# Compressing cache rows: a feature-major copy in SBUF between the loaded rows and TensorE, keys and values in turn

## The chip, the cores and the metric

The kernel runs on one core of a Trainium2 chip. The metric is the device time of one execution in microseconds; before the change it is 1770.71 us, the median of three runs (1770.42 to 1772.65). The profile shows one further execution.

## The reference

One inference step of a two-layer decoder: a prompt of 512 tokens and 8 sample tokens with 2048 past positions each share all weights. Layer 0 is sparse attention with three branches (compressed blocks, selected blocks, a window), layer 1 gated linear attention; each is followed by a SwiGLU feed-forward. The part at hand is the compression of the cached rows of the 8 samples. Each cached row holds 4 heads of 64 features for keys and as many for values; 64 consecutive rows make a block, and each block is reduced to one row a head:

```python
def compress_blocks(rows, pe, w1, w2):
    B, L = rows.shape[:2]
    nb = L // CMP_BLK                                   # CMP_BLK = 64
    blk = rows[:, :nb * CMP_BLK].reshape(B, nb, CMP_BLK, 2, NSA_KV_HEADS, NSA_HEAD_DIM)
    h = jax.nn.silu(jnp.einsum('bnlcgd,lcde->bncge', blk + pe[:, :, None, :], w1))
    return jnp.einsum('bncge,cef->bncgf', h, w2)

# for each sample: 2048 rows gathered by page_table, 16 pages of 128 rows
cmp_past = cache_cmp_kv[li, page_table].reshape(B, past_len, 2, G, D)
ckv = concatenate([compress_blocks(cmp_past, pe, w1, w2), compress_blocks(cmp_kv, pe, w1, w2)])
```

The prompt's own rows (8 blocks) are compressed with the same weights. The results feed a small attention, whose probabilities also choose the selected blocks.

## The kernel before

Phases follow one another, each a block of instruction streams, one for each engine, with semaphores between them: the projection (`phase_project`), the compression (`phase_compress`), the attention over compressed rows (`phase_cmp_attention`), the selected and window attention (`phase_attention`), then the trunk of layer 0, layer 1 and its trunk. At the end of a block all engines meet.

The compression has 128 pages (8 samples of 16), each with keys and values. It works in eight units `UN`: 32 pages (`ROW_UNIT`) of keys four times, then 32 pages of values four times. A page of one kind is 128 rows of 256 floats: position in the partition, 1 KB a partition and page. A unit is 32 such pages side by side. TensorE multiplies, for each of the 64 features d, the 64 positions of a block (in partitions 0 to 63 and, for the second block of a page, 64 to 127) by the 64x64 weights `w1[:, c, d]`, and adds over d in PSUM. The moving operand for one d is one element of each page and head: 128 columns which lie 64 floats apart (`flat`, line 704). Features 0 to 31 go to one half of the output partitions and 32 to 63 to the other (`far`), blocks to two banks (`hf`), so that four 64x64 matmuls stand in four tiles of the array at a time. A unit is 32 steps of four matmuls (256 records in the trace, since a float32 matmul shows as two). Some units carry extra columns: four for the position row `pe`, in the first unit of keys and of values (132), 16 for the prompt's rows, in the second of each (144, with the unused four).

Two row buffers alternate: `rows0`, whose first 32 pages are loaded during the projection, and a second. The load of unit n + 2 waits for `conv_done` of unit n. The 32 page DMAs are issued by SyncE (13), ScalarE (10) and GpSimd (9) (`ROW_SHARE`), each with a page number read from the page table into a register (`row_pages`, line 105), for each unit anew.

After a unit VectorE adds the two halves and the position term (`other`, `pre`), ScalarE takes the sigmoid (`sig`), VectorE multiplies (`hid`). Within the last unit's convolution, between steps of TensorE, the prompt's blocks are finished: second weights for them (`new_blocks`), `prompt_values`, `prompt_scores`, `turn_scores`, and on VectorE the prompt's softmax (`prompt_softmax`), which there stands ahead of the last unit's activation. The product of all `hid` with the second weights `w2` (line 718) ends the phase.

`xT`, the transposed input of 128 x 8 x 520 floats (2.13 MB), stays in SBUF through all of this, from the projection to the trunk of layer 0, though no phase between reads it. In the projection weights stream through four slots `raw`; SyncE's queue issues them, and GpSimd's `low_done` frees a slot.

## Time and profile before

| what | value |
|---|---|
| median of three runs | 1770.71 us |
| the profiled execution | 1766.21 us, of it a span of 1764.5 us |
| mean granted clock of TensorE over the span | 0.959 |
| first convolution matmul of the compression | 173.96 us after the span's start |
| first product with the second weights | 314.09 us |
| first matmul of the compressed attention | 317.35 us |
| TensorE busy over the span | 92% |

The profile's times count from the span's start. "PE" is TensorE's matmuls, "PEld" its weight loads, DVE VectorE, ACT ScalarE, POOL GpSimd, SP SyncE; a "q" behind an engine is its instruction queue. "L709" is a line of the kernel. In a timeline, neighbouring instructions of one line are merged, and the bracket says how long the engine was idle before them and what released it. The granted clock is a share of 2.4 GHz and takes two levels, 1.00 and 0.50 (1.2 GHz).

### The profile page before, as it was taken

To read this page: it belongs to the slowest core of one execution; us is meant where nothing else is said; L and a number is where in the kernel's file an instruction comes from. 1 tells how busy PE (TensorE), PEld (TensorE's weight loads), DVE (VectorE), ACT (ScalarE), POOL (GpSimd) and SP (SyncE) were. 2 spreads that over 40 slices of the span, in tenths; PEclk is the share of its full clock that TensorE was granted. 3 is DMA by queue.
4 is the path that set the end of the run, shared out by engine and by line. 5 is a ranking of instruction groups with operands and counts; after the bars stand their busy time and mean duration, and the time that the engine had idled before them with its cause. 6 is when DMAs were issued, how large, how long until landed. Compare 5 with 4: busy or idle time off the path is not lost. (4 is left out here: it accounts for less than half of the span.)

```text
span 1764.5 us, 35479 instructions
## 1 busy us (share of the span) xinstructions
PE 1631.3 (92%) x13658; PEld 1429.0 (81%) x13658; DVE 729.4 (41%) x1364; ACT 577.6 (33%) x1142; POOL 723.1 (41%) x503
## 2 busy tenths in 40 slices
PE   6998889698899888999999999998979999999997
PEld 6998777476666677999999988987658899999996
DVE  2111011555455669332232267136659523223234
ACT  3221001255454435422222224126534532222323
POOL 6641231343255446644344336412126644434420
PEclk9999999799999999999999999998979999999998
DMA  8326885255454543533333222324223333333211
GB/s 211 103 80 170 282 271 162 75 181 155 139 162 149 152 120 120 167 120 108 110 119 96 84 64 69 99 83 155 61 71 109 96 110 93 91 89 99 85 32 49
DMA packets 297280, 211.42 MB, mean 120 GB/s; under 512 B 34148, under 2 KB 290328, under 8 KB 296600
## 3 DMA queue, kind: packets, MB, share of 16 engines
q1 hardware_dynamic: 279000, 175.69, 33.4%
q0 software_dynamic: 7552, 20.06, 3.6%
q10 hardware_dynamic: 10560, 13.41, 2.8%
q8 instruction: 109, 1.79, 0.4%
q14 instruction: 59, 0.48, 0.1%
HBM read 199.02 MB, written 18.42 MB: 123 GB/s over the span
## 5 line engine op out<-in xcount | busy, mean ns | idle before, releaser
L1670 POOL TENSOR_TENSOR w_low_t<-w_raw,w_high_t 128x1024 fp32r<-128x1024 f32 (+1 forms) x126 | 298.7, 2380 | 296.3 <-ACT w_high_t L1778 296.3
L1511 PE MATMUL ps<-x_parts,w_high_t 128*128 128x512 f32 x720 | 262.5, 403 | 16.3 <-POOL w_low_t L1670 15.7
L1758 PE MATMUL ps<-x_parts,w_high_t 128*128 128x264 f32 x720 | 205.1, 285 | 0.0
L1760 PE MATMUL ps<-x_parts,w_low_t 128*128 128x264 f32 x720 | 204.4, 284 | 0.0
L1759 PE MATMUL ps<-x_parts,w_high_t 128*128 128x264 f32 x720 | 204.4, 284 | 0.0
L1513 PE MATMUL ps<-x_parts,w_low_t 128*128 128x256 f32 x720 | 204.3, 284 | 0.0
L1511 PEld LDWEIGHTS ps<-x_parts,w_high_t 128*128 128x128 f32 x720 | 138.2, 192 | 47.9 <-POOL w_low_t L1670 16.5
L1778 ACT CAST w_high_t<-w_raw 128x1024 fp32r<-128x1024 f32 (+1 forms) x126 | 127.9, 1024 | 135.6 <-PE ps L1760 118.3
L1670 POOL TENSOR_TENSOR w_low_ahead<-w_raw,w_high_ahead 128x1024 fp32r<-128x1024 f32 (+1 forms) x40 | 95.1, 2380 | 132.2 <-ACT w_high_ahead L1778 132.2
L1513 PEld LDWEIGHTS ps<-x_parts,w_low_t 128*128 128x128 f32 x720 | 138.5, 192 | 0.1
L1758 PEld LDWEIGHTS ps<-x_parts,w_high_t 128*128 128x128 f32 x720 | 135.4, 188 | 2.9
L1759 PEld LDWEIGHTS ps<-x_parts,w_high_t 128*128 128x128 f32 x720 | 135.4, 188 | 0.1
L1760 PEld LDWEIGHTS ps<-x_parts,w_low_t 128*128 128x128 f32 x720 | 135.3, 188 | 0.0
L709 PE MATMUL ps<-rows,w 64*64 64x128 f32 (+2 forms) x2048 | 118.3, 401 | 17.7 <-DMA rows<-in_cache_cmp 12.3
L709 PEld LDWEIGHTS ps<-rows,w 64*64 64x64 f32 x2048 | 97.7, 157 | 37.8 <-issue 15.1
L1078 POOL TENSOR_TENSOR e<-e,rg 128x1024 f32<-128x1024 f32 (+3 forms) x48 | 66.9, 1394 | 113.4 <-DVE rg L1332 113.0
L1912 DVE TENSOR_REDUCE whole_t<-ps 128x256 f32<-128x512 f32 x44 | 30.4, 690 | 181.4 <-PE ps L1513 181.4
L328 PE MATMUL ps<-x_parts,pw_high 128*128 128x260 f32 x320 | 93.4, 292 | 5.2 <-POOL pw_low L248 5.2
L1795 ACT CAST hid_parts<-h_t 128x256 fp32r<-128x256 f32 (+1 forms) x88 | 36.1, 410 | 186.3 <-DVE h_t L1917 186.3
L1511 PE MATMUL ps<-hid_parts,w_high_t 128*128 128x512 f32 x264 | 93.8, 395 | 0.0
L329 PE MATMUL ps<-x_parts,pw_high 128*128 128x260 f32 x320 | 91.0, 284 | 0.0
L330 PE MATMUL ps<-x_parts,pw_low 128*128 128x260 f32 x320 | 90.6, 283 | 0.0
(392 smaller groups left out, 3914.0 us busy)
## 6 DMA issues: line engine op xcount, KB each, us to landing
w_raw<-in_ffn_w_gu SPq DMA_DIRECT2D x88, 512.0 KB, 3.7
pages<-in_cache_slc SPq DMA_DIRECT2D x192, 128.0 KB
rows<-in_cache_cmp SPq DMA_DIRECT2D x123, 128.0 KB, 5.5
w_raw<-in_ffn_w_down SPq DMA_DIRECT2D x32, 448.0 KB, 3.7
w_raw<-in_gla_w_in SPq DMA_DIRECT2D x24, 512.0 KB, 3.7
rows<-in_cache_cmp ACTq DMA_DIRECT2D x70, 128.0 KB, 6.2
pages<-in_cache_slc POOLq DMA_DIRECT2D x64, 128.0 KB, 2.9
w_raw<-in_ffn_w_down SPq DMA_DIRECT2D x16, 512.0 KB, 4.0
```

The lines of the kernel that those rows point to most:

```text
L328: nc.tensor.matmul(out, high[:, u % SLOTS, k, :], X[0][:, k, c], start=(k == 0), stop=False)
L329: nc.tensor.matmul(out, high[:, u % SLOTS, k, :], X[1][:, k, c], start=False, stop=False)
L330: ins = nc.tensor.matmul(out, low[:, u % SLOTS, k, :], X[0][:, k, c], start=False, stop=(k == KT - 1))
L709: ins = nc.tensor.matmul(ps[64 * far:64 * far + 64, 2 * (n % 2) + hf, 0:m * G], w1[half, c, d + D // 2 * far, :], flat[half, d + D // 2 * ...
L1078: nc.gpsimd.tensor_tensor(part, part, rg[:, n % 4].unsqueeze(2).to_broadcast([P, 2, w]), ALU.mult)\
L1511: nc.tensor.matmul(bank[:, 0:2 * FOLD].rearrange("p (a n) -> p a n", a=2), high, parts[2][:, :, at, 0:FOLD], start=(k == 0), stop=False)
L1513: return nc.tensor.matmul(bank[:, FOLD:2 * FOLD], low, parts[0][:, at, 0:FOLD], start=False, stop=(k == n - 1))
L1670: nc.gpsimd.tensor_tensor(low(u)[:, 0:k], raw[:, u % RAW, 0:k], high(u)[:, 0:k].bitcast(F32), ALU.subtract).then_inc(low_done, 1)
L1758: nc.tensor.matmul(psum(i), high(u)[:, k, :], a[0][:, at, c], start=(k == 0), stop=False)
L1759: nc.tensor.matmul(psum(i), high(u)[:, k, :], a[1][:, at, c], start=False, stop=False)
L1760: ins = nc.tensor.matmul(psum(i), low(u)[:, k, :], a[0][:, at, c], start=False, stop=(k == t.kc - 1))
L1778: nc.scalar.copy(high(u)[:, 0:k], raw[:, u % RAW, 0:k]).then_inc(high_done, 1)
```

## The change

Between the row buffers and TensorE stands a ring of four small tiles `flat`. ScalarE and VectorE in turn copy chunks into it: a chunk is 4 features of each half for all 128 columns, feature outermost, so that the columns of one feature are neighbours. A unit has 8 chunks (`CH`, a local name here); even ones are ScalarE's, odd ones VectorE's (`flatten`). TensorE waits for each chunk and releases it with `chunk_done`. Prompt rows and position rows are copied into the chunks of the first two units by the same engines, as 16 columns and one.

The order of units is keys, values, keys, values of the same pages, so page numbers are read once for two units. A row buffer is free when all its chunks are copied. The shares of the page issues are 14, 6 and 12. ScalarE's issues of its part stand behind its copies of a unit. VectorE's work on unit n - 1 stands among its copies for unit n, and the prompt's work is spread over units 3 to 6.

Three of the four ring tiles lie where `xT` was. So `xT` is written to DRAM (`x_saved`) in the projection, behind the issue of the fifth unit's weights, and read back at the end of the attention's page loads, ahead of the trunk's first weights on the same queue.

```diff
-ROW_SHARE = (0, 13, 23, ROW_UNIT)
+ROW_SHARE = (0, 14, 20, ROW_UNIT)
@@ phase_project, SyncE: in the loop over weight units u
                 if u == SPREAD0 - 1:
+                    sp.wait_ge(xT_done, 2 * NT)
+                    sp.dma_start(S["x_saved"], xT[:].rearrange("p k t -> p (k t)")).then_inc(xT_saved, 16)
                     sp.wait_ge(pt_in, 16)
-                    for hf in range(2):
-                        sp.dma_start(S["rows0"][64 * hf:64 * hf + 64, 32], io["nsa_pe_cmp"][0, :, 0, :].unsqueeze(1)
-                                     .to_broadcast([BLK, G, D])).then_inc(cst["rows0_in"], 16)
@@ phase_project, ScalarE: behind the loads of w1
+            for c in range(2):
+                for hf in range(2):
+                    act.dma_start(S["pe_cmp"][64 * hf:64 * hf + 64, c], io["nsa_pe_cmp"][0, :, c, :]).then_inc(cst["rows0_in"], 16)
@@ phase_compress
-    UN = [(c, p) for c in range(2) for p in range(PARTS)]
-    EX = (1, PARTS + 1)
+    UN = [(c, p) for p in range(PARTS) for c in range(2)]
+    EX = (0, 1)
+    PEC = COLS + XC
+    CD, RING = 4, 4
+    CH = D // 2 // CD
@@ load_part
             if n >= 2:
-                eng.wait_ge(conv_done, n - 1)
+                eng.wait_ge(flat_act, CH // 2 * (n - 1))
+                eng.wait_ge(flat_dve, CH // 2 * (n - 1))
...
+            if n % 2 and n + 1 < len(UN):
+                S["next_pages"][by] = row_pages(eng, S, (n + 1) // 2, by)
+        def flatten(eng, copy, n, j, done):
+            c, k = UN[n][0], CH * n + j
+            dst = flat[k % RING]
+            if j < 2:
+                rows_there(eng, n)
+            if k >= RING:
+                eng.wait_ge(chunk_done, k - RING + 1)
+            if n in EX:
+                for f in range(2):
+                    src = S["cmpn"][:, 0:TILES, c * G * D:(c + 1) * G * D].rearrange("p t (g e) -> p e t g", g=G)
+                    copy(dst[:, f, :, COLS:COLS + XC].rearrange("p e (t g) -> p e t g", g=G),
+                         src[:, f * (D // 2) + CD * j:f * (D // 2) + CD * (j + 1)])
+                copy(dst[:, :, :, PEC], S["pe_cmp"][:, c].rearrange("p (f e) -> p f e", f=2)[:, :, CD * j:CD * (j + 1)])
+            src = rows[n % 2][:].rearrange("p s g (f e) -> p f e (s g)", f=2)
+            copy(dst[:, :, :, 0:COLS], src[:, :, CD * j:CD * (j + 1), :]).then_inc(done, 1)
@@ ScalarE
+            for n in range(len(UN)):
+                for j in range(0, CH, 2):
+                    flatten(act, nc.scalar.copy, n, j, flat_act)
+                    if j == 2 and n:
+                        sigmoid(n - 1)
+                if n == 6:
+                    act.wait_ge(e_ready, 1)
+                    nc.scalar.activation(sp_[:], sp_[:], ACT.Exp, scale=SCALE).then_inc(e_done, 1)
+                if n == 0:
+                    load_part(act, 1, 1, rows_act)
+                    for c in range(2):
+                        act.dma_start(w2[64 * c:64 * c + 64], io["nsa_w_cmp2"][0, c]).then_inc(w2_in, 16)
+                    for name in ("pm_add", "pm_01"):
+                        act.dma_start(S[name][:], io[name + "_tab"]).then_inc(pm_in, 16)
+                if n + 2 < len(UN):
+                    load_part(act, n + 2, 1, rows_act)
+                if n == 4:
+                    act.wait_ge(cst["cmp_out"], 16 * 4)
+                    act.wait_ge(flat_dve, CH // 2 * len(EX))
                     for g in range(G):
                         act.wait_ge(sT_done, g // 2 + 1)
                         nc.scalar.copy(sT[:, g], ps[:, 4 + g, :]).then_inc(sT_ready, 1)
+            sigmoid(len(UN) - 1)
@@ VectorE
+            for n in range(len(UN)):
+                for j in range(1, CH, 2):
+                    flatten(dve, nc.vector.tensor_copy, n, j, flat_dve)
+                    if j == 1 and n:
+                        activate(n - 1)
+                    if j == 3 and n:
+                        finish(n - 1)
+                    if j == 3 and n == 4:
+                        new_values()
+                if n == 3:
+                    new_keys()
+                if n == 5:
+                    shift_scores()
+                if n == 6:
+                    prompt_softmax()
@@ TensorE
+            beside = {(3, 4): new_blocks, (4, 0): prompt_values, (4, 6): prompt_scores, (5, 2): turn_scores}
             for n, (c, p) in enumerate(UN):
...
+                for j in range(CH):
+                    k = CH * n + j
+                    if (n, j) in beside:
+                        beside[n, j]()
+                    pe.wait_ge(flat_dve if j % 2 else flat_act, k // 2 + 1)
+                    for e in range(CD):
+                        for far in range(2):
+                            for hf in range(2):
+                                half = slice(64 * hf, 64 * hf + 64)
+                                ins = nc.tensor.matmul(ps[64 * far:64 * far + 64, 2 * (n % 2) + hf, 0:m],
+                                                       w1[half, c, CD * j + e + D // 2 * far, :], flat[k % RING][half, far, e, 0:m],
+                                                       start=(j == 0 and e == 0), stop=(j == CH - 1 and e == CD - 1),
+                                                       tile_position=(64 * hf, 64 * far))
+                    ins.then_inc(chunk_done, 1)
@@ phase_attention, SyncE: behind all page loads
+            sp.dma_start(S["xT"][:].rearrange("p k t -> p (k t)"), S["x_saved"]).then_inc(xT_back, 16)
             sp.wait_ge(sc_done, NK)
             for u in range(RAW):
                 load_unit(sp, cst["raw"], cst["w_in"]["t0"], u, next_units[u])
+            sp.wait_ge(xT_back, 16)
```

SyncE now issues the tables behind all of its page loads. `activate` and `finish` are the two halves of the former work after a unit; their operations are the same.

## Rows read from the trace of the kernel before

**Rows 1.** The page: busy time, share of the span and instructions of each engine.

```profile
PE 1631.3 (92%) x13658; PEld 1429.0 (81%) x13658; DVE 729.4 (41%) x1364; ACT 577.6 (33%) x1142; POOL 723.1 (41%) x503
```

**Rows 2.** Timeline of TensorE, 173 to 315 us: start, length, operation, count, idle before.

```profile
173.96 14.60 PE L709 MATMUL ps<-rows,w 64*64 64x132 f32 x256 [3.33 <-PEq L123]
195.45 29.90 PE L709 MATMUL ps<-rows,w 64*64 64x144 f32 x512 [6.89 <-DMA rows<-in_cache_cmp]
...
227.83 14.17 PE L709 MATMUL ps<-rows,w 64*64 64x128 f32 x256 [2.48 <-DMA rows<-in_cache_cmp]
...
243.45 14.66 PE L709 MATMUL ps<-rows,w 64*64 64x132 f32 x256 [1.45 <-DMA rows<-in_nsa_pe_cmp]
...
258.78 15.87 PE L709 MATMUL ps<-rows,w 64*64 64x144 f32 x256 [0.67 <-issue]
...
291.83 1.99 PE L709 MATMUL ps<-rows,w 64*64 64x128 f32 x32 [2.46 <-DMA rows<-in_cache_cmp]
...
305.15 5.44 PE L709 MATMUL ps<-rows,w 64*64 64x128 f32 x96
314.09 1.61 PE L718 MATMUL ps<-hid,w 64*64 64x512 f32 x8 [3.50 <-DVE hid L644]
```

**Rows 3.** Windows: length, busy time (records) of PE to POOL, granted clock, DMA.

```profile
197.00:198.00 1.00, 1.00 (x24) 1.00 (x20) 0.00 (x0) 0.00 (x0) 0.00 (x0) 0.50 1.10 366
...
200.00:201.00 1.00, 1.00 (x24) 0.87 (x20) 0.00 (x0) 0.00 (x0) 0.00 (x0) 1.00 1.03 325
```

**Rows 4.** Windows of line 718: length, PE, PEld, clock, DMA share, GB/s.

```profile
314.10:314.15 0.05, 0.05 (x4) 0.05 (x6) 1.00 0.00 0
...
314.50:314.55 0.05, 0.05 (x4) 0.00 (x0) 0.73 0.00 0
...
314.60:314.65 0.05, 0.05 (x8) 0.00 (x0) 0.50 0.00 0
```

**Rows 5.** DMA view of 173.8 to 195.4 us; timeline of ScalarE's queue.

```profile
DMA packets 5949, 7.11 MB, mean 329 GB/s; under 512 B 870, under 2 KB 5495, under 8 KB 5909
...
211.59 6.05 ACTq L504 DMA_DIRECT2D rows<-in_cache_cmp  x10
```

**Rows 6.** Groups by line and form: count, busy us, mean ns, idle before.

```profile
L352 ACT CAST pw_high<-w_raw 128x1024 fp32r<-128x1024 f32 x20 | 21.0, 1052 | 1.2 <-DMA w_raw<-in_nsa_w_in 1.2
...
L623 DVE COPY rows<-cmpn 128x256 f32<-128x256 f32 x8 | 1.8, 284 | 0.6 <-PEq L123 0.6
...
L434 DVE COPY qs<-qT 64x32 f32<-64x32 f32 x8 | 1.1, 185 | 0.0
```

**Rows 7.** Line 105: duration min/median/max ns; timeline of the queue of ScalarE.

```profile
L105 ACTq TENSOR_LOAD <-pt x70: 271/275/714, 159.1 to 269.9; - x70
L105 ACTq FUSED_REGOPS  x70: 147/147/170, 159.8 to 270.2; - x70
...
179.12 3.68 ACTq L547 DMA_DIRECT2D w<-in_nsa_w_cmp  x2
```

**Rows 8.** Timeline of VectorE at the phase's end.

```profile
311.46 0.69 DVE L610 TENSOR_TENSOR p_cmp<-p_cmp,sm_p 128x512 f32<-128x512 f32 x1
312.19 0.42 DVE L633 COPY c_other<-ps 64x256 f32<-64x256 f32 x1
```

**Rows 9.** The projection: windows; timelines of SyncE's queue and of ScalarE.

```profile
24.00:28.00 4.00, 4.00 (x33) 4.00 (x33) 0.00 (x0) 0.00 (x0) 4.00 (x5) 0.95 1.08 346
...
40.00:44.00 4.00, 4.00 (x32) 3.88 (x31) 1.40 (x2) 1.54 (x2) 1.51 (x2) 1.00 0.65 193
...
27.22 1.01 SPq L209 DMA_DIRECT2D w_raw<-in_nsa_w_in  x2
...
41.67 1.05 ACT L352 CAST pw_high<-w_raw 128x1024 fp32r<-128x1024 f32 x1
```

**Rows 10.** The attention's end: timeline of SyncE's queue; tile w_raw, 560 to 660 us.

```profile
589.04 51.20 SPq L1525 DMA_DIRECT2D w_raw<-in_nsa_w_out  x32
...
L1778 ACT CAST w_high_t<-w_raw x7: 1030/1040/1050, 625.5 to 659.8; 128x1024 fp32r<-128x1024 f32 x7
```

More of the change, by code:

```diff
@@ L237, in _ @@
             sp.wait_ge(kv_out, 16 * 8)
+            sp.wait_ge(xT_saved, 16)
         @block.gpsimd
@@ L468, in sem @@
             return cst["sems"].new(name)
-        rows = (S["rows0"], sb("rows", [P, QP + EXTRA, G, D]))
+        rows = (S["rows0"], sb("rows", [P, QP, G, D]))
+        flat = [nc.alloc_sbuf_tensor_at("flat%d" % i, [P, 2, CD, WIDE], F32, offset=S["xT_at"] + 8 * CD * WIDE * i)
+                for i in range(RING - 1)] + [sb("flat%d" % (RING - 1), [P, 2, CD, WIDE])]
         w1 = S["w1"]
```

160 lines of the change are left out of this document (63 added, 97 removed).

## The prediction

> **What bounds the kernel now.** I read the page's shares first: TensorE is busy for 92% of the span [rows 1], but that is an average over phases. The change touches one, the compression, so I took the timeline of that stretch next. TensorE's first convolution matmul there starts at 173.96 us, the last ends at 305.15 + 5.44 = 310.6, and the product with the second weights, which ends the phase for TensorE, starts at 314.09 [rows 2]. So the phase lasts 140.1 us. A unit (32 pages of keys or of values) takes 14.2 us with 128 columns, 14.6 with 132, 15.9 with 144; between units TensorE waits 6.89, 2.48, 1.45, 0.67 and 2.46 us, mostly for rows from DRAM (the second and third units follow without a wait, the seventh nearly so) [rows 2]. TensorE is thus busy most of the phase, and some 14 us are waits.
>
> Is a unit's 14.2 us bounded by TensorE's clock? Each float32 matmul shows as two records, so a unit is 256 records, or 64 groups of four that lie in four different 64x64 tiles of the array. A group takes 14.2 / 64 = 222 ns with 128 columns and 15.87 / 64 = 248 ns with 144: 1.6 ns for each further column, and nearly nothing left over. So columns set the pace, not weight loads. But the pace doesn't follow the clock: at a granted clock of 0.50 (1.2 GHz) as many matmuls are in flight per microsecond as at 1.00 (2.4 GHz), 24 and 24 [rows 3], and the second unit, which began at the low clock, took 29.90 - 14.2 = 15.7 us against 15.87 for its like at the full one [rows 2]. What streams is the strided operand: neighbours lie 64 floats apart. The same 64x64 tiling with a contiguous operand stands at the phase's end, 512 columns: four matmuls are in flight from 314.10 to 314.55 and eight, the next four with them, from 314.60, nearly all of it at the full clock [rows 4]. That is 0.45 to 0.5 us for 512 columns, 0.88 to 0.98 ns a column, about half of 1.7. So the bound is the strided read, and reading contiguously at the full clock should give 113 to 125 ns a group, 7.2 to 8.0 us a unit. At the low clock it doubles the 0.88, but no more than the present 14.2, since the rows of the strided form at that clock already hold that pace.
>
> The Trainium skill (SBUF — State Buffer, the note on cachelines in the section on the DMA port swizzle) says that accesses which each touch a new 16-byte line pay a penalty. By that rule the trace's 222 ns are explained; it gives no size for float32 on TensorE, so the sum goes by the rows above.
>
> **The change, step by step.**
>
> *TensorE's columns.* Both first units now carry 145 columns; of the others none exceeds 128. At the present pace this is 2 x 145 + 6 x 128 against 2 x 132 + 2 x 144 + 4 x 128: 1058 against 1064 columns, nothing. With the halved cost, units fall from 14.2 to between 7.2 and 14.2 us. After a wait the clock is low at first (it was 0.50 from before the second unit's start until about 198.5 [rows 3]), for 3 us at least; with half of that lost I take 9.5 us.
>
> *DMA becomes the pace.* A unit is 32 pages of 131 KB, 4.19 MB. In the stretch from 173.8 to 195.4 the DMAs moved 7.11 MB at 329 GB/s [rows 5], which gives 12.7 us for a unit with the queues full. A unit's load that stands alone, with its ramp, took from 211.59 (ACT's first issue) to 227.83 (TensorE's start), 16.2 us, some 0.5 MB of tables in it [rows 2, 5]. Now loads hardly overlap, since a buffer is free only when the unit's convolution is over. Afterwards a buffer is free when its rows are in the ring, which runs up to four of eight chunks ahead, and the other load is then under way. I take 13.5 us a unit when two loads overlap and 15 for one alone; the ends are 12.7 and 16.2.
>
> *The copies.* A chunk is 1024 elements a partition. ScalarE's nearest row is the cast of 1024 contiguous ones, 1.05 us; VectorE copied 256 within SBUF in 0.28 us and moves 32 strided ones in 0.185 [rows 6]. A strided copy of 1024 isn't shown: from below 1.05 us; from above twice that, if the stride costs it what it costs TensorE. Four chunks per engine and unit are 4.2 to 8.4 us, beside TensorE and the loads. I take 1.1 (ScalarE's pace of about 1 ns an element leaves more room than TensorE's). In the first two units two or three small copies are added to each chunk, 0.2 us each: 1.7.
>
> *ScalarE's queue.* This is where the change adds waits. ScalarE copies even chunks, and its six page issues of the load after next stand between its copies of one unit and of the next. Ten issues took 6.05 us [rows 5], so six take about 3.5; six page numbers take 0.275 + 0.147 us and gaps each [rows 7], 3.3 in all, now once in two units. If ScalarE is late, the next unit's first chunk is, and TensorE behind it. In the first unit it is worst: its part of load 1 was issued at 173.9, and now comes only behind its copies; then come two w2 issues (3.68 us before [rows 7]), two mask tables and its part of load 2, before it may copy a row of unit 1.
>
> *The walk.* Unit 0: first chunk at 175.6, and ScalarE's last copy (it needs TensorE to be through chunk 2, at the low clock) ends at 182.5. Then 3.5 + 3.3 + 3.7 + 3.7 + 3.5 gives 200.2 for the first copy of unit 1, while TensorE, done at about 185, waits 16 us (6.9 before). Copies of unit 1 end 8.5 us later, 208.7; ScalarE is through with its issues at 215.5, where unit 2's copies start (its rows, issued by 200, are there), ending at 222.5. Load 3 started at 208.7 and lands at 223.7; unit 3 starts at 226. Load 4 started at 222.5 and lands at 237.5; loads 5, 6 and 7 follow by 13.5 us: 278. Then 1.1 for a copy and 9.5 for TensorE: 288.6, where before it was 310.6. TensorE's side work (new blocks, prompt scores, turning), which lengthened the last unit to 310.6 - 291.8 = 18.8 us, lies in waits of the fourth to sixth units and costs nothing; without that cover it is 18.8 - 14.2 = 4.6 us.
>
> *The tail.* The softmax held VectorE until 312.15, so the last activation began 1.6 us after TensorE's end; then come 1.9 us until 314.09 [rows 8]. Now the softmax is over a unit earlier: 288.6 + 2.0 = 290.6. Gain: 314.1 - 290.6 = 23.5 us.
>
> *x to DRAM and back.* 2.13 MB, 6.5 us at 329 GB/s, each way. Out: behind the fifth unit's weights at 22.5 us, in a stretch where DMA is nearly full (1.08 between 24 and 28) and has room only later (0.65 between 40 and 44). The sixth unit's weights were issued at 27.22 and ScalarE took them up at 41.67, 14 us later [rows 9]; 6.5 us fit in, and the two broadcasts of position rows are gone. Without that cover it costs up to 6.5. Back: queued behind the last pages at 589 us, ahead of weights that are first read at 625.5 [rows 10]: hidden. Four small issues on ScalarE in the projection replace four page numbers. I put 0.3 us for all of it.
>
> *The sum.* The profiled run took 1766.2 us, its span 1764.5. 1766.2 - 23.5 + 0.3 = 1743; the median of the three runs is 4.5 us above the profiled one, so 1770.7 - 23.2 = 1747.5, rounded to 1747.
>
> **Rivals.**
>
> *TensorE stays at 14.2 us a unit.* For it: no row shows eight instructions in 115 ns over a long run, and a TensorE that waits between units may spend them at the low clock, where 128 contiguous columns take what they take now. Then unit 1 starts at 201 and ends at 217; six more, 85, and 4.6 of side work give 307, with the tail 309: a gain of 5, 1766 us. Against it: four 64x64 matmuls started together in rows 4. The Trainium skill (TensorE: Matmul & The Clock Gate, the section on HAM oscillation) warns of just this, DMA waits between bursts that put the clock down each time; here it would give the 1766, and the rows of the low clock after the 6.89 us wait agree that the clock falls.
>
> *Copies or ScalarE's queue set the pace.* At 2.1 us a copy ScalarE needs 8.4 + 3.5 + 1.7 + 0.5 for a unit, 14.1, and copies wait on chunks on top; with 15 us a unit from 222 the end comes at 222 + 5 x 15 + 11 = 308 at worst, 300 if half overlaps: 6 to 14 us, about 1760.
>
> *Slower.* One mechanism: the copy out of the strided rows costs 3 us or more, because VectorE and ScalarE pay the stride harder than TensorE. Then 12 + 5.7 = 17.7 us a unit, over the present 16.3 to 16.8 between starts: 200 + 7 x 17.7 + 4 = 328, 14 us slower, 1785. It decides from about 2.7 us a copy. The 0.185 us for 32 strided elements speaks against it, since most of that is fixed.
>
> *Nothing is left.* The first rival with x's way out uncovered: 5 us gained and up to 6.5 lost, 1771 at most and within 0.2%.
>
> **How the numbers follow.** Forecast 57%, 1747, its own range 1738 (12.7 us a load) to 1756 (16.2 for some of them). TensorE unchanged 15%, 1766. Copies or queue 16%, 1760. Slower 6%. Cancelling 6%. A measurement here can tell about 0.2%, 3.5 us. Faster by more than that: 0.87; within: 0.07; slower: 0.06. The range that leaves out 2 in 10 goes from 1736 to 1766.
>
> **What would show it.** Right: convolution units of 7 to 10.5 us of TensorE time; waits between units that end on copies, which waited for rows; DMA share near 1 from 222 on; a first wait of TensorE of some 15 us; the second-weights product some 117 us after 173.9, not 140. Wrong: units of 13 us or more; ScalarE's copies of 2 us; TensorE in the projection waiting for weights near 40 us; a later start of the trunk's first product.

## The result, and the profile after

The changed kernel takes 1759.65 us (median of 5 runs, 1755.05 to 1766.01) where the kernel before takes 1770.71 (5 runs, 1769.48 to 1772.65): a ratio of 0.9943, 95% interval 0.9926 to 0.996. That is 11.1 us faster, less than half of the 23.7 that were forecast, and it is the time of the rival "copies or ScalarE's queue set the pace", 1760, which had been given 16%. The profiled execution took 1758.1 us with a span of 1756.4, so the two profiles differ by 8.1 us, three less than the medians do.

TensorE's share falls by one point from that in [rows 1], its busy time by 38 us:

```profile
PE 1593.4 (91%) x13658; PEld 1407.0 (80%) x13658; DVE 757.8 (43%) x1412; ACT 643.3 (37%) x1198; POOL 740.8 (42%) x522
```

The timeline of TensorE through the compression, which answers to [rows 2] (start, length, operation, count, idle before):

```profile
183.68 9.88 PE L755 MATMUL ps<-flat,w 64*64 64x145 f32 x256 [12.46 <-ACT flat L539]
204.39 9.77 PE L755 MATMUL ps<-flat,w 64*64 64x145 f32 x256 [10.82 <-ACT flat L539]
220.35 9.89 PE L755 MATMUL ps<-flat,w 64*64 64x128 f32 x256 [6.19 <-ACT flat L539]
...
290.06 5.21 PE L755 MATMUL ps<-flat,w 64*64 64x128 f32 x128 [1.55 <-ACT flat L539]
295.52 3.89 PE L755 MATMUL ps<-flat,w 64*64 64x128 f32 x128 [0.26 <-ACT flat L539]
301.38 1.09 PE L765 MATMUL ps<-hid,w 64*64 64x512 f32 x8 [1.97 <-DVE hid L675]
```

A run of 256 records is again a unit. It now takes 9.8 to 9.9 us, and 128 records at the full clock take 3.89, which makes 3.89 / 32 = 122 ns a group of four records in place of 222 (the prediction's group is four records; a step of four matmuls is eight): the halving came as forecast. But each unit waits, and on a copy, not on rows. The product with the second weights stands at 301.38 where it was at 314.09: 12.7 us of the forecast 23.5. The reason is seen on ScalarE. Its timeline over the same stretch, where `ACTq` is its queue of DMA issues:

```profile
181.10 0.50 ACT L535 COPY flat<-cmpn 128x64 f32<-128x64 f32 x2 [9.90 <-DMA pe_cmp<-in_nsa_pe_cmp]
...
201.84 0.49 ACT L535 COPY flat<-cmpn 128x64 f32<-128x64 f32 x2 [10.61 <-issue]
...
211.96 2.96 ACTq L511 DMA_DIRECT2D rows<-in_cache_cmp  x6
218.30 3.77 ACT L539 COPY flat<-rows 128x1024 f32<-128x1024 f32 x2 [6.50 <-issue]
...
227.63 3.82 ACTq L511 DMA_DIRECT2D rows<-in_cache_cmp  x6
231.64 3.82 ACT L539 COPY flat<-rows 128x1024 f32<-128x1024 f32 x2 [4.17 <-issue]
...
287.98 3.85 ACT L539 COPY flat<-rows 128x1024 f32<-128x1024 f32 x2 [1.58 <-DMA rows<-in_cache_cmp]
```

Two copies together take 3.77 to 3.85 us in these rows. With units counted from 0 to 7: behind the fourth copy of a unit, ScalarE issues six pages of the load after next (3 to 4 us), reads page numbers in every second unit, and only then starts on the next unit. So its first copies of units 2 and 3 come at 218.30 and 231.64, with idle times that end on "issue" and not on rows. Between its first copies of unit 1 and of unit 7 it waited for rows once, for 1.58 us. It also waited for TensorE and VectorE there, 4.04 us in unit 4 (for the prompt's scores) and 3.57 at the start of unit 6; of 6.79 idle us ahead of unit 4, which the view puts down to TensorE, half are page numbers. The copies by line and form, ScalarE's and VectorE's of the same shape and the same number (count, busy us, mean ns, idle before):

```profile
L539 ACT COPY flat<-rows 128x1024 f32<-128x1024 f32 x32 | 62.4, 1973 | 27.6 <-PE ps L755 11.7 <-issue 10.7 <-DVE flat L539 3.6
...
L539 DVE COPY flat<-rows 128x1024 f32<-128x1024 f32 x32 | 33.9, 1058 | 18.5 <-PE ps L755 14.2 <-DMA rows<-in_cache_cmp 4.2
```

1973 ns on ScalarE, 1058 on VectorE. And the windows of that stretch, in which the DMA share (last but one column, the granted clock ahead of it) should have been near 1 from 222 us on:

```profile
201.00:208.00 7.00, 3.61 (x64) 3.64 (x68) 0.52 (x2) 6.17 (x13) 0.00 (x0) 0.51 1.03 337
...
222.00:229.00 7.00, 6.93 (x197) 6.68 (x193) 3.02 (x5) 4.50 (x4) 0.84 (x2) 0.79 0.66 205
...
236.00:243.00 7.00, 4.60 (x145) 4.26 (x141) 3.10 (x9) 3.56 (x2) 2.61 (x5) 0.92 1.06 349
```

It is 0.66 at 222 to 229 and 1.06 at 236 to 243, falls to 0.74 at 250 to 257 again, and its mean from 222 to 278 is 0.88, for the loads start when the copies are through and these are late. The first unit began late as well: 181.10 against the forecast 175.6. The tile with the rows of positions, its issues and landings:

```profile
L385 ACTq DMA_DIRECT2D pe_cmp<-in_nsa_pe_cmp x4: 618/618/628, 160.0 to 162.0; - x4
...
DMA to landing us min/median/max: 19.0/19.2/19.8
```

They are issued at 160.0 to 162.0 on ScalarE's queue behind the first weights, 4.2 MB, and land 19 us later.

**Behind the phase** part of the gain goes again. "The trunk's second layer" is here the first product that reads the hidden values of the trunk's feed-forward (`hid_parts`). The start of TensorE's same matmuls in the two profiles, before against after: product with the second weights 314.09 and 301.38 (12.7 us earlier); the attention's last product 622.75 and 612.09 (10.7); the trunk's first 629.04 and 618.68 (10.4); the trunk's second layer 775.54 and 767.98 (7.6); the end 8.1. Attention has one new wait, 1.2 us for pages of the window cache; such waits come and go, kernel 1 below, without x's trip, has one of 1.4 us for other pages. The trunk's first layer, from its first product to the second layer's, takes 149.3 us in place of 146.5 and waits for nothing new. What differs is seen in windows around its longest wait, for the squares of the normalisation. Of before and after, first the timeline row of the wait, then windows of 3 us (length, PE, PEld, DVE, ACT, POOL, clock, DMA share, GB/s):

```profile
694.73 0.71 PE L1704 MATMUL ps<-ln_sq_t,mean_mat 128*128 128x264 f32 x2 [2.79 <-DVE ln_sq_t L1960]
```

```profile
692.00:695.00 3.00, 0.27 (x1) 0.27 (x2) 2.93 (x5) 0.00 (x0) 0.02 (x1) 1.00 0.77 227
695.00:698.00 3.00, 3.00 (x18) 2.58 (x18) 1.73 (x4) 2.03 (x3) 0.00 (x0) 1.00 0.04 10
```

```profile
685.59 1.19 PE L1753 MATMUL ps<-ln_sq_t,mean_mat 128*128 128x264 f32 x2 [2.81 <-DVE ln_sq_t L2009]
```

```profile
683.00:686.00 3.00, 0.41 (x1) 0.41 (x2) 2.93 (x5) 0.00 (x0) 0.00 (x0) 0.95 0.69 194
686.00:689.00 3.00, 3.00 (x10) 2.40 (x10) 1.59 (x4) 2.16 (x4) 0.00 (x0) 0.50 0.02 6
```

The wait is the same, 2.79 and 2.81 us. Before, the clock granted behind it is 1.00 and TensorE gets through 18 matmuls in 3 us; after, it is 0.50 (1.2 GHz) and 10 matmuls. So what differs behind this wait is the clock, not the work.

### The profile page after: what moved, and what is told of

Its sections match the earlier page's. It is cut to its first block and busy times, and to the rows that moved or that the text cites. A ratio compares the mean times of both kernels' runs of the same rounds, so it can differ in the third digit from the quotient of the medians.

```text
span 1756.4 us, 35338 instructions
## 1 busy us (share of the span) xinstructions
PE 1593.4 (91%) x13658; PEld 1407.0 (80%) x13658; DVE 757.8 (43%) x1412; ACT 643.3 (37%) x1198; POOL 740.8 (42%) x522
## 5 line engine op out<-in xcount | busy, mean ns | idle before, releaser
L1827 ACT CAST w_high_t<-w_raw 128x1024 fp32r<-128x1024 f32 (+1 forms) x126 | 127.9, 1024 | 136.6 <-PE ps L1809 118.3
L755 PE MATMUL ps<-flat,w 64*64 64x128 f32 (+1 forms) x2048 | 76.8, 314 | 47.5 <-ACT flat L539 43.7
L755 PEld LDWEIGHTS ps<-flat,w 64*64 64x64 f32 x2048 | 72.8, 158 | 51.8 <-issue 48.2
```

Of the source, the lines that this page charges most:

```text
L755: ins = nc.tensor.matmul(ps[64 * far:64 * far + 64, 2 * (n % 2) + hf, 0:m], w1[half, c, CD * j + e + D // 2 * far, :], flat[k % RING][half ...
L1827: nc.scalar.copy(high(u)[:, 0:k], raw[:, u % RAW, 0:k]).then_inc(high_done, 1)
```

## The experiments

Each of the twelve kernels was timed beside the kernel before on the same chip, and the ratios are to that kernel before. Kernels 1 to 4, 5 to 8, 9 to 11, and 12 ran on four different chips, so kernels of different groups are compared by their ratios; 0.001 of a ratio is 1.8 us. "The product" is that with the second weights, at 314.09 us before and 301.38 after.

**1. The kernel before, read contiguously.** TensorE reads the rows where they lie, so the wrong elements meet the weights; sizes and counts are those of before.

```diff
-flat = rows[n % 2][:, 0:m].rearrange("p s g d -> p d (s g)")
+flat = rows[n % 2][:, 0:m].rearrange("p s g d -> p (s g d)")\
+    .rearrange("p (d x) -> p d x", d=D)
```

> The kernel before, with one edit: TensorE reads each unit's rows as if they lay feature by feature, so 128 contiguous floats where it read 128 floats 64 apart. The elements are the wrong ones for their feature (that part of the result is changed), the instructions, loads, buffers and waits are those of before. Theory A, the strided read is what bounds TensorE: a unit falls from 14.2 us to 7.2 at the full clock and 9 to 10 with the low clock after each wait; the loads then set the pace, and since a load only starts when the buffer's convolution is over, a pair of units takes a load (16 us) and a convolution (9 us) at least, so 13 us a unit and more; the phase (140 us) shrinks by 15 to 25 us. Rival B, TensorE's instructions or weight loads take 14 us anyway: units stay at 14 us and the phase at 140.

1763.49 us (6 runs), ratio 0.996, 0.9943 to 0.9977. Timeline of TensorE, all runs of 512 records:

```profile
200.38 17.10 PE L709 MATMUL ps<-rows,w 64*64 64x144 f32 x512 [15.19 <-DMA rows<-in_cache_cmp]
232.58 16.99 PE L709 MATMUL ps<-rows,w 64*64 64x128 f32 x512 [15.10 <-DMA rows<-in_cache_cmp]
264.94 16.83 PE L709 MATMUL ps<-rows,w 64*64 64x144 f32 x512 [15.38 <-DMA rows<-in_cache_cmp]
...
311.57 1.98 PE L718 MATMUL ps<-hid,w 64*64 64x512 f32 x8 [6.07 <-DVE hid L644]
```

Two units take 17 us where they took 28 to 30, in a kernel in which nothing else was touched: the strided read was the bound. But each pair now waits 15 us for rows, the pairs stand 32.3 us apart, and the product comes 2.5 us earlier, no more. The expectation had the phase shrink by 15 to 25 us, which missed. So halving TensorE's work alone is worth 7.5 us in the medians and 1.9 in the profiles' spans; a unit's load that starts when TensorE is through with the buffer takes as long as before. What the ring adds to the faster read is that it lets the buffers go early.

**2. The trip of x alone.** The kernel before, with x saved to DRAM behind the fifth weight unit and fetched back ahead of the trunk's weights, as in the change.

```diff
 if u == SPREAD0 - 1:
+    sp.wait_ge(xT_done, 2 * NT)
+    sp.dma_start(S["x_saved"], xT[:]...).then_inc(xT_saved, 16)
...
     load(sp, i, range(SP_B), in_sp)
+sp.dma_start(S["xT"][:]..., S["x_saved"]).then_inc(xT_back, 16)
 sp.wait_ge(sc_done, NK)
```

> The kernel before, and only the way of x to DRAM and back is added, at the places where the change has it; x also stays in SBUF. Prediction: 0.3 us. Theory A, the trip costs what the trace of the changed kernel hints at behind the compression: 1 us of a late last window page in the attention and up to 3 us in the trunk's first units: 2 to 5 us slower than before. Rival B, it is hidden and those 4.6 us come from elsewhere: within 1 us of before.

1773.26 us (12 runs) against 1770.96 (25 runs), ratio 1.0014, 1.0004 to 1.0024: the trip costs 2.5 us, 0.7 to 4.2. I had put 0.3 for it. The two transfers of 2080 KB took 12.5 and 14.4 us here, not 6.5. In the one profile the product comes 3.6 us later than before, at 317.67, and the trunk's first layer takes 149.9 us for 146.5; its span is 7.4 us longer, three times what the medians say, so these parts are not the price of the trip one by one.

**3. The trip at another place.** The changed kernel, with the save behind the fourteenth weight unit and the fetch among attention's page loads.

```diff
-sp.wait_ge(xT_done, 2 * NT)
-sp.dma_start(S["x_saved"], ...)          # behind the fifth unit
+if u == 13:
+    sp.dma_start(S["x_saved"], ...)
...
 load(sp, i, range(SP_B), in_sp)
+if i == DEPTH + 4:
+    sp.dma_start(S["xT"][:]..., S["x_saved"])
```

> The changed kernel, with x written to DRAM behind the fourteenth weight unit instead of the fifth, and read back among the attention's page loads (behind the fifth load of that loop) instead of ahead of the trunk's first weights. If the trip as placed costs 3 to 5 us (theory A), this is 2 to 5 us faster than the changed kernel's 1759.65, about 1756; if it is hidden (rival B), 1759 to 1760.

1762.71 us (12 runs), ratio 0.9961, 0.9949 to 0.9972: no gain over the changed kernel, so moving the trip to this place saves nothing. The twelve runs tell something else. They go from 1753.95 us at a mean granted clock of 0.955 to 1769.0 at 0.942, and nearly in order (a correlation of -0.94 over the twelve), some 1.2 us for each 0.001 of the clock, 15.05 / 13. The 25 runs of the kernel before on that chip have clocks of 0.954 to 0.959 and times without such an order (-0.2). This is a correlation; no run here sets the clock by itself.

**4. The rows of positions ahead of the first weights**, in the changed kernel.

```diff
+for c in range(2):
+    for hf in range(2):
+        act.dma_start(S["pe_cmp"][...], io["nsa_pe_cmp"]...)
 for c in range(2):
     for hf in range(2):
         act.dma_start(w1[...], io["nsa_w_cmp1"]...)
```

> The changed kernel, with the four small loads of position rows issued on ScalarE's queue ahead of the four loads of the first weights (4.2 MB) instead of behind them. Theory A, the ring's first copies wait for the position rows because these stand behind all first weights: the first copy moves from 181.1 to about 175 us, the phase ends 6 us earlier, about 1754. Rival B, something behind it (the load of unit 1, ScalarE's queue) is due at the same time: the first convolution starts earlier and the second does not, under 2 us gained in all.

1759.6 us (6 runs), ratio 0.9937, 0.9919 to 0.9955: nothing. The first copy does come at 174.29 and TensorE starts 7 us earlier, at 176.87. Timeline of ScalarE, then of TensorE:

```profile
205.02 0.50 ACT L535 COPY flat<-cmpn 128x64 f32<-128x64 f32 x2 [20.42 <-DMA rows<-in_cache_cmp]
```

```profile
176.87 7.34 PE L755 MATMUL ps<-flat,w 64*64 64x145 f32 x163 [5.68 <-ACT flat L539]
...
207.60 10.07 PE L755 MATMUL ps<-flat,w 64*64 64x145 f32 x256 [19.27 <-ACT flat L539]
```

The second unit starts 3 us later than in the changed kernel. Its rows, ScalarE's six pages issued at 182.3 to 186.3, are there only at 205; the third unit's pages, let go by earlier copies, were by then under way as well (ScalarE's issued from 192.02 on, where the changed kernel has 197.54). The product stands at 305.70, 4.3 us later than in the changed kernel. The late rows of positions were an error of my walk, but not a cost.

**5. VectorE makes all copies**, ScalarE keeps the activations, its page numbers and its issues.

```diff
-for j in range(0, CH, 2):
-    flatten(act, nc.scalar.copy, n, j, flat_act)
-    if j == 2 and n:
-        sigmoid(n - 1)
+if n:
+    sigmoid(n - 1)
...
-for j in range(1, CH, 2):
+for j in range(CH):
     flatten(dve, nc.vector.tensor_copy, n, j, flat_dve)
```

> The changed kernel, with VectorE copying all eight chunks of a unit (1.06 us each in the changed kernel's trace) and ScalarE none (1.97 us each); ScalarE keeps its page issues, sigmoids and exponential. Theory A, ScalarE sets the pace of 14.3 us a unit with four copies, six issues and every second time six page numbers: units then follow at 13 us or less, TensorE's wait before unit 1 ends when its rows land (195.7 instead of 202), and the phase, which ends at 301.4 in the changed kernel, ends at 285 to 291; about 1747 us. Rival B, the loads set the pace: at most 3 us faster than the changed kernel's 1759.65.

1751.43 us (4 runs), ratio 0.9899, 0.9883 to 0.9916, clear of the changed kernel's 0.9926 to 0.996, though short of the 1747 expected. The product comes at 292.58, 21.5 us earlier than before and 2 us from the prediction's 290.6. Groups, then windows:

```profile
L538 DVE COPY flat<-rows 128x1024 f32<-128x1024 f32 x64 | 65.0, 1053 | 18.2 <-DMA rows<-in_cache_cmp 17.2 <-PE ps L752 0.9
```

```profile
215.00:222.00 7.00, 4.80 (x131) 4.08 (x126) 5.03 (x7) 0.00 (x0) 2.57 (x4) 0.90 1.05 350
222.00:229.00 7.00, 3.53 (x78) 3.31 (x74) 1.83 (x2) 0.00 (x0) 6.27 (x11) 0.74 1.04 329
```

VectorE alone copies a unit in 8 x 1.05 = 8.4 us, which is below what a load takes, and now waits for rows; the DMA share is 1.05 and 1.04 where the changed kernel has 1.00 and 0.66, and TensorE no longer waits over 5 us from the second unit on. The edit moves the sigmoid as well, which no longer stands behind copies: VectorE waited 25.9 us for it in the changed kernel (13.1 and 12.8) and waits 0.9 here. There is a price too: GpSimd's twelve page issues of a unit, which took 7.5 to 8.6 us from the first to the last, take 8.0 to 16.1 us; why is not shown. Taking half of the copies from an engine whose queue was full is worth more than sharing them out.

**6. ScalarE issues its pages later**, behind its second copy of the next unit, in the changed kernel.

```diff
     if j == 2 and n:
         sigmoid(n - 1)
+        if n + 1 < len(UN):
+            load_part(act, n + 1, 1, rows_act)
...
-if n + 2 < len(UN):
-    load_part(act, n + 2, 1, rows_act)
```

> The changed kernel, with ScalarE's page issues for the load after next standing behind its second copy of the next unit, not ahead of its first. Same work on ScalarE in another order. If ScalarE is saturated (theory A), TensorE's waits move into the unit and the pace stays at 14.3 us, within 2 us of the changed kernel. If only the order holds TensorE up (rival C), its waits of 2.5 to 6.2 us before units shrink to 1 to 2 and the phase ends 6 to 10 us earlier.

1755.03 us (4 runs), ratio 0.992, 0.9901 to 0.994, which overlaps the changed kernel's 0.9926 to 0.996. The product comes at 300.56, 0.8 us earlier. ScalarE's first copy of the second unit comes 4.8 us sooner (197.07 for 201.84), but in the units behind it the copies wait again on issue, 6.22 us before 220.82, and on late rows, 2.67 before 210.28: the queue is as full as before, only in another order.

**7. ScalarE copies contiguously**: its large copies read 1024 neighbours (the wrong elements), VectorE's stay strided.

```diff
+if j % 2 == 0:
+    src = rows[n % 2][:].rearrange("p s g d -> p (s g d)")\
+        .rearrange("p (f e x) -> p f e x", f=2, e=D // 2)
+else:
-src = rows[n % 2][:].rearrange("p s g (f e) -> p f e (s g)", f=2)
+    src = rows[n % 2][:].rearrange("p s g (f e) -> p f e (s g)", f=2)
```

> The changed kernel, with ScalarE's large copies reading their 1024 elements contiguously (the wrong elements, so half of the compressed sums are changed); VectorE's copies read as before. Theory A, the strided read doubles ScalarE's copy: 1.97 us falls to 1.05, four copies save 3.7 us a unit, and the pace falls from 14.3 to 12.7 to 13.5 us, the phase by 5 to 9 us. Rival: the 1.97 us come from something else (the four-dimensional shape, or the port shared with DMA writes): it stays above 1.5 us and nothing is gained.

1754.67 us (4 runs), ratio 0.9915, 0.9898 to 0.9931; this interval too touches the changed kernel's. Groups by line and form, then ScalarE's timeline:

```profile
L542 DVE COPY flat<-rows 128x1024 f32<-128x1024 f32 x32 | 33.9, 1060 | 29.5 <-PE ps L758 19.9 <-DMA rows<-in_cache_cmp 9.5
L542 ACT COPY flat<-rows 128x1024 f32<-128x1024 f32 x32 | 32.8, 1045 | 44.2 <-PE ps L758 20.3 <-issue 12.6 <-DMA rows<-in_cache_cmp 11.2
```

```profile
216.52 1.99 ACT L542 COPY flat<-rows 128x1024 f32<-128x1024 f32 x2 [7.40 <-issue]
...
229.45 1.99 ACT L542 COPY flat<-rows 128x1024 f32<-128x1024 f32 x2 [5.24 <-issue]
```

The same engine, size and destination take 1045 ns instead of 1973: the stride doubles ScalarE's copy. The product comes at 296.19, 5.2 us of the 8.8 that taking ScalarE's copies away brings. What is left is mostly the queue: 7.40 and 5.24 us of "issue" ahead of a unit's first copies, and from 216.52 to 229.45 a unit still takes 12.9 us.

**8. The same as 5, with pages shared 11, 11 and 10** among the queues of SyncE, ScalarE and GpSimd, not 14, 6 and 12.

```diff
-ROW_SHARE = (0, 14, 20, ROW_UNIT)
+ROW_SHARE = (0, 11, 22, ROW_UNIT)
```

> As e5_all_dve, and the page issues dealt as 11, 11 and 10 instead of 14, 6 and 12, since ScalarE has room. Theory A: once ScalarE's copies are gone the issue of 32 pages and the reading of page numbers are spread evenly, a load's last page is issued 2 us earlier, 0 to 4 us better than e5_all_dve. If the bytes alone bind then: the same as e5_all_dve.

1756.68 us (5 runs), ratio 0.9937, 0.9913 to 0.996, the product at 300.00: 7.4 us worse than kernel 5 in the phase; in the times the two intervals just touch. The pages do come sooner, and VectorE waits 7.1 us for rows where it waited 21.4. But it now waits for the sigmoid, which stands behind ScalarE's longer row of issues and page numbers. VectorE's waits from 176 to 300 us (what it waits for: us in total, times, longest):

```profile
DVE hid L672 <- ACT c_sig L563: 9.9, 5, 4.7
DVE hid L670 <- ACT c_sig L563: 7.7, 1, 7.7
```

That is 17.6 us where kernel 5 has 0.9. ScalarE's free time isn't worth giving to page issues as long as the sigmoid stands behind them; with the sigmoid ahead of them it wasn't tried.

**9 and 10. All copies on VectorE, and the rows of positions first**; in 10 the trip of x is also moved as in 3.

```diff
 (the edits of 5 and 4; in 10 those of 3 too)
```

> VectorE makes all copies, and the four rows of positions are loaded ahead of the first weights. Theory A (with ScalarE's copies gone, ScalarE's page numbers and issues of the second unit no longer stand behind copies, so the earlier start of the first unit is kept): the first copy moves from 180.3 to about 174 us and the second weights' product from 292.6 to 286-289; 1746 to 1749 us, a ratio of 0.986 to 0.988. Theory B (the loads set the pace of the whole phase, at about 330 GB/s from 205 us on, and nothing that starts earlier than them counts): the product stays at 291-294 and the time at 1750 to 1753 us, 0.989 to 0.990.

> The same as the last, and x is saved behind the fourteenth weight unit and fetched back among attention's page loads. Theory A (the fetch beside the trunk's first weights costs the trunk's first layer 3 us, as its distance from the trunk's first product to the second layer's first product says: 149.7 us against 146.5 before, and 146.6 where the trip was moved alone): that distance falls to 146.5 and the time lies 2 to 3 us below the last kernel's. Theory B (a fetch among attention's loads costs attention as much): the distance falls, but attention's 309.8 us from the second weights' product to its last product grow by 2 to 3 us, and the time is the last kernel's.

1762.18 us (6 runs), ratio 0.9947, 0.9929 to 0.9964, and 1764.05 us (11 runs), 0.9968, 0.9957 to 0.9979. The expectations missed: the edit that was worth nothing in 4 costs 8.5 us here by the ratios, 0.9947 for 0.9899 (10.8 by the medians of two chips), and 12.4 us in the phase. Timelines of kernel 9, VectorE and then TensorE:

```profile
204.14 0.36 DVE L534 COPY flat<-cmpn 128x64 f32<-128x64 f32 x2 [19.53 <-DMA rows<-in_cache_cmp]
```

```profile
205.66 6.49 PE L752 MATMUL ps<-flat,w 64*64 64x145 f32 x128 [18.60 <-DVE flat L538]
...
304.93 1.51 PE L762 MATMUL ps<-hid,w 64*64 64x512 f32 x8 [1.98 <-DVE hid L672]
```

The second unit's rows are there at 204, where kernel 5, which began 6 us later, had them at 195.12. The first unit's early end lets the third unit's pages in at once (ScalarE's at 184.78, in kernel 5 at 191.11), among the second's. The mean DMA share from 201 to 278 us is 0.84 for kernel 5's 0.95. In kernel 10 the product stands at 305.23 and the trunk's first layer takes 149.5 us, as without the move.

**11. ScalarE loads no pages** in the changed kernel; SyncE takes its six beside its fourteen.

```diff
-ROW_SHARE = (0, 14, 20, ROW_UNIT)
+ROW_SHARE = (0, 20, 20, ROW_UNIT)
```

> The kernel after, but ScalarE loads no pages of the compression: SyncE takes its six beside its fourteen. Theory A (ScalarE's queue of about 14 us a unit is 8 us of copies and some 6 of issues and page numbers, and both count): a unit falls to 10 to 12 us and the second weights' product comes at 285-293 us instead of 301.4; 1749 to 1754 us, a ratio of 0.988 to 0.991. Theory B (the transfers themselves, not their issue, set 13 us a unit once the issues are out of the way): the product comes at 296-301 us, and the time is 1754 to 1759 us, 0.991 to 0.994.

1768.84 us (10 runs), ratio 0.9991, 0.9981 to 1.0002: the whole gain is gone. Waits from 170 to 312 us (engine, tile and line, what it waits for: us in total, times, longest), then windows:

```profile
ACT flat L539 <- DMA rows<-in_cache_cmp: 48.2, 3, 18.2
DVE flat L539 <- DMA rows<-in_cache_cmp: 46.6, 3, 17.8
```

```profile
229.00:236.00 7.00, 7.00 (x259) 6.78 (x254) 5.03 (x7) 6.97 (x5) 4.66 (x5) 1.00 0.32 95
...
264.00:271.00 7.00, 5.76 (x171) 3.95 (x160) 3.32 (x5) 5.28 (x7) 4.90 (x8) 1.00 0.36 105
```

Neither expectation held. The issues left ScalarE, but the rows are late instead: both copying engines wait up to 18 us for them, every second unit, while the DMA engines stand at 0.32 and 0.36 between. SyncE's own program shows why. Its loads of page numbers in the first of these gaps (line 104; duration min/median/max ns, first and last start):

```profile
L104 SPq TENSOR_LOAD <-pt x20: 261/267/276, 228.4 to 239.2; - x20
```

Twenty page numbers take it 11 us, and it issues no page meanwhile. The forty issues of two units take 24.8 us, 203.2 to 228.0. That makes 36 us for two units, and two units do take 35.4, from 221.58 to 256.99, the first copies behind these waits. SyncE waits for nothing in this stretch, and its pages land 3.8 us behind their issue (median from 190 to 300 us), sooner than in the changed kernel (6.7). So it isn't that one queue brings twenty pages slowly: SyncE's turn of issues and page numbers, 18 us a unit, has become the pace, as ScalarE's was before. The issues were work that had to be dealt out; only ScalarE's copies could be taken away from it at a gain.

**12. Kernel 9, and the third unit's loads wait until the second's have landed.**

```diff
     eng.wait_ge(flat_dve, CH * (n - 1))
+if n == 2:
+    for q, arrived_q in enumerate((rows_sp, rows_act, rows_sw)):
+        eng.wait_ge(arrived_q[1], 16 * (SHARE[q + 1] - SHARE[q]))
```

> The kernel in which VectorE makes all copies and the rows of positions come ahead of the first weights (1762.2 us), with one edit: the loads of the third unit wait until those of the second have landed. Theory A (the earlier first unit let the third unit's pages into the queues while the second's were under way, and these landed at 203.7 us in place of 195, since both shared the DMA engines): the second unit's first copy comes at 190 to 196 us in place of 204.1, the second weights' product at 286 to 294 in place of 304.9; 1744 to 1752 us, a ratio of 0.985 to 0.990. Theory B (the second unit's pages are late because the first weights share the DMA engines with them, until about 182 us, and they would be so in any order): the first copy stays at 200 to 205 us, and the third unit's rows come later than before, so the product stands at 304 to 310; 1760 to 1766 us, 0.994 to 0.998.

1761.96 us (6 runs), ratio 0.9952, 0.994 to 0.9964. VectorE's timeline:

```profile
197.38 0.37 DVE L537 COPY flat<-cmpn 128x64 f32<-128x64 f32 x2 [12.63 <-DMA rows<-in_cache_cmp]
...
219.88 1.99 DVE L541 COPY flat<-rows 128x1024 f32<-128x1024 f32 x2 [10.04 <-DMA rows<-in_cache_cmp]
...
250.33 2.00 DVE L541 COPY flat<-rows 128x1024 f32<-128x1024 f32 x2 [10.25 <-DMA rows<-in_cache_cmp]
```

Half an answer. The second unit's rows are there at 197.38 and not at 204.14, so 6.8 us of the delay did come from the third unit's pages; the last 2 us to kernel 5's 195.12 didn't, and stay open. But the third unit's rows then come at 219.88, 22.5 us behind the second's, and the product stays at 304.86. From there on loads go out in pairs: GpSimd issues the 24 pages of two units in one go at 198.06, 230.58 and 260.81 us, where in kernel 5 it issues them twelve at a time, and VectorE waits 10.04, 10.25 and 6.37 us for the first unit of each pair and not for the second. The mean DMA share from 201 to 278 us is 0.89, for 0.95 in kernel 5 and 0.84 in kernel 9. My reading, which no run tests by itself: what makes kernel 5 good is not an early start but that a load is nearly always under way and the next one joins it late.

## Why the prediction was wrong

**The step that failed is the term of the copies**, "I take 1.1 (ScalarE's pace of about 1 ns an element leaves more room than TensorE's)". It measured 1.97 us on ScalarE and 1.06 on VectorE. I had kept both ends, 1.05 and 2.1, and chose the lower one for both engines from a row of ScalarE with contiguous elements; VectorE had a row with a stride [rows 6], ScalarE none, and the only engine whose strided pace a row showed, TensorE, paid double. Kernel 7 shows the doubling on ScalarE by itself, 1973 to 1045 ns. With 1.97 ScalarE's turn is 4 x 1.97 + 3.5 of issues + 1.7 of page numbers + 0.4 of the activation = 13.5 us before any wait on a chunk, as long as the longer price of a load, 12.7 to 13.5; measured were 14.1 from unit 3 to unit 7, (287.98 - 231.64) / 4. The rival had said 14.1 for copies of 2.1 us.

How much of the miss is this term? Of the 10.8 us that the phase fell short, 301.38 - 290.6, kernel 7, whose copies take what the forecast had, gives back 5.2. Kernel 5, with no copy on ScalarE at all, gives back 8.8, and 8.2 us of time, 1759.65 - 1751.43. So a smaller step failed beside it, **the walk of ScalarE's queue**: it let unit 3 start 10.5 us behind unit 2, at 226, with 7 us for the copies and 3.5 for the issues. In kernel 7, with short copies, 12.9 us lie between the two and unit 3 starts at 229.45, because ScalarE waits for chunks among its copies and its first copies of a unit come 7.40 and 5.24 us late on "issue". From there to the product kernel 7 takes 66.7 us, where the walk had 64.6. The last 2.0 us are missing in kernel 5 too.

**Where the 10.8 us of the phase went**, along my walk: first copy of unit 1 at 201.84 for 200.2 (1.6); of unit 2 at 218.30 for 215.5 (1.2 more); of unit 3 at 231.64 for 226 (2.8 more); of unit 7 at 287.98 for 278 (4.3 more); the last unit and the tail 13.4 us for 12.6 (0.8). Of these, the second to fourth lie in the stretch that ScalarE's turn paces; from unit 4 on its waits for TensorE and VectorE are in them as well, and the runs don't part the two. That the first is so small is luck, as told below.

**TensorE's columns: right.** 122 ns a group at the full clock for a forecast of 113 to 125; units of 9.8 us for 9.5. Kernel 1 shows it with nothing else changed. The rival by which TensorE stays at 14.2 fell, and with it what I had drawn from the Trainium skill (TensorE: Matmul & The Clock Gate, the section on HAM oscillation) in favour of it: the clock does go down behind the long waits, as that section says (0.51 in the window from 201 to 208 us), but a contiguous unit spends only its first part there: the unit that began at 204.39 is back at 1.00 by 208. The rule that the Trainium skill gives on cachelines (SBUF — State Buffer, the note in the section on the DMA port swizzle) agrees with kernels 1 and 7, where TensorE and ScalarE pay about double for 256-byte strides. VectorE shows no such price: 1058 ns for 1024 strided elements against 284 for 256 contiguous ones [rows 6], four times which is 1136; a contiguous copy of 1024 was not run on it.

**The walk's start: wrong, and made good by luck.** I had the first copy at 175.6 and overlooked that the rows of positions now come through a queue behind 4.2 MB of weights; it came at 181.10. ScalarE's last copy of unit 0 ended at 191.22 for a forecast 182.5. Yet its first copy of unit 1 came only 1.6 us late, since the walk had the queue's other terms too high: the first load's issues went out beside the last copy, and the w2 issues and the two tables took 1.15 and 1.1 us for 3.7 and 3.7. So 8.7 us late and 7.1 us saved cancelled. The wait of 10.82 us before the second unit, for a forecast 16, is the other side of it. Kernel 4 took the delay away and got nothing back.

**DMA as the pace: wrong in this kernel, nearly right in kernel 5.** The share was to be near 1 from 222 us on; it is 0.66 in the first window there and 0.88 on the mean to 278 us. With ScalarE's copies gone it is 1.04 and 0.97, and the product comes at 292.58 for a forecast 290.6.

**The tail: right.** 301.38 - (295.52 + 3.89) = 2.0 us, as forecast.

**x's trip: mis-sized.** 0.3 us forecast, 2.5 (0.7 to 4.2) measured by kernel 2. Moving it gained nothing, as kernel 3 shows; that its transfers take 12 to 14 us and not 6.5 is seen, what they hold up is not.

**Behind the phase** I had nothing, and 4.6 us went, 12.7 - 8.1 in the profiles. With the 10.8 of the phase, less the 0.3 put for the trip, that is the 15.1 us between the 1743 of the sum and the 1758.1 of the profiled run; in the medians 12.6 are missing. 1.2 are a page wait in attention; 2.8 are the trunk's first layer. It lasts 149.2 to 149.9 us in nine of the twelve profiles of kernels with the trip (the changed one, 2, 4 to 10), 146.5 to 146.8 in three (3, 11, 12), and 146.5 and 146.6 in the two without (before and kernel 1). In all fourteen the wait for the squares is 2.8 us long. In the five short ones the 3 us behind it are granted 1.00, in the nine long ones 0.50 to 0.56. So a kernel with the trip has the short layer when it has the clock. Each kernel has one profile, and only two are without the trip, so whether the trip has a part in the clock is not shown. Why the same wait puts the clock down in most profiles of the newer kernels stays open. The Trainium skill describes such a fall behind waits (TensorE: Matmul & The Clock Gate, the section on HAM oscillation), but the wait is the same in both groups here.

## What to carry to other kernels

A copy that turns a stride into contiguous memory is priced engine by engine, each from a row of that engine with that stride. Where there is none, both bounds stay in the sum: here TensorE's doubling held for ScalarE and not for VectorE. Add up the whole turn of each engine that both computes and issues transfers, with its issues and register reads, and compare it with the transfer's pace. Here it was 13.5 us against 12.7 to 13.5, and moving the four copies of 2 us to an engine with room was worth 8.2 us beside the 11.1 of the whole change. The same sum explains kernel 11 (18 us for SyncE's issues and page numbers) and points at kernel 8 (a sigmoid behind eleven issues and page numbers). And look at what an earlier start lets into the queues: kernels 9 and 12, beside 5, suggest that two loads which go out together serve worse than two that are staggered.

## What the runs showed of the hardware

- A strided float32 read (neighbours 256 bytes apart) costs TensorE 222 ns for four records of 128 columns, half of what four matmuls show, with 24 records a us at a granted clock of 0.50 and of 1.00 [rows 3]; a contiguous one costs 122 ns at the full clock. ScalarE takes 1973 ns against 1045 for 1024 elements a partition, VectorE 1058 with the stride.
- One 2080 KB transfer between SBUF and DRAM took 9.6 to 14.7 us in these kernels, 145 to 222 GB/s, while all queues together moved 350 GB/s in a window of kernel 5.
- An engine that issues 20 page loads a unit and reads 20 page numbers for every second one needs 18 us a unit (24.8 us for 40 issues, 11 for 20 numbers), and the DMA engines fell to 0.32 and 0.36 while it read. With 14, 6 and 12 pages on three engines they stood at 0.74 to 1.08 from 201 to 278 us in kernel 5.
- While VectorE made all copies (kernel 5), GpSimd's twelve page issues of a unit took 8.0 to 16.1 us; in the changed kernel they took 7.5 to 8.6.
- One kernel's time varied by 15 us in twelve runs, in step with its mean granted clock (0.942 to 0.955), and the same wait of 2.8 us is followed by the full clock in five profiles and by half of it, or nearly (0.50 to 0.56), in nine; these are profiles of different kernels, one each.
